# Second attention block: the last V chunk and the first output units cut in halves and placed between the head pairs, Q and K transposed into four PSUM banks each, scores in one pair of banks

## What is computed

```python
q, k, v = jnp.split(h @ w_qkv, 3, axis=-1)            # h 256 x 1024, w_qkv 1024 x 3072
q = rms_norm_2(to_heads(q), q_norm_g); k = rms_norm_2(to_heads(k), k_norm_g)   # 16 heads of 64
s = einsum(q, k) / 8 - slope[head] * dist             # causal: -inf above the diagonal
out = softmax(s) @ v                                  # 256 tokens are one block: plain causal attention
return out @ w_o                                      # w_o 1024 x 1024
```

## Time and profile before

| | us |
|---|---|
| median of 3 runs (lowest, highest) | 1060.16 (1060.11, 1060.77) |
| the profiled execution, its own time | 1060.12 |
| its span, first to last instruction | 1058.3 |
| PE busy in the span | 1030.8 (97%) |
| DVE, ACT, POOL busy | 712.5, 496.4, 110.3 |
| first Q transpose | at 789.40 |
| first scores, last values of a head pair | at 809.00, at 852.29 |
| last output matmul starts | at 864.18 |

### The profile page before, as it was taken

How to read it: one execution, slowest core, us unless ns; L and a number is a source line. 1 busy time by engine, 2 the same in 40 slices (tenths; PEclk the granted TensorE clock), 3 DMA queues, 4 the chain that set the end, 5 groups by cost and what they waited for, 6 DMA issues and landing times.

```text
span 1058.3 us, 16734 instructions
## 1 busy us (share of the span) xinstructions
PE 1030.8 (97%) x6774; PEld 907.4 (86%) x6774; DVE 712.5 (67%) x877; ACT 496.4 (47%) x565; POOL 110.3 (10%) x81
## 2 busy tenths in 40 slices
PE   8999998999999999999999999999997899999998
PEld 8987776799999998986899999998876689999997
DVE  6868646887667778754887656778674566545563
ACT  6455436454344436431564344436454655443440
POOL 1040002000010002025000010000000401000010
PEclk9999999899999999999999999999999899999999
DMA  8974346639787883694539778882652425655541
GB/s 320 371 261 141 120 127 218 236 110 345 260 274 281 272 279 126 203 288 133 194 134 350 269 265 284 268 282 92 238 162 78 159 81 199 192 191 179 193 160 40
DMA packets 119019, 221.62 MB, mean 209 GB/s; under 512 B 6510, under 2 KB 21040, under 8 KB 118960
## 3 DMA queue, kind: packets, MB, share of 16 engines
q1 hardware_dynamic: 117152, 214.97, 59.9%
q0 software_dynamic: 1680, 5.79, 1.7%
q10 hardware_dynamic: 128, 0.03, 0.0%
HBM read 215.07 MB, written 1.05 MB: 204 GB/s over the span
## 4 chain that ended last, share of the span: by engine, by line
PE 86%; DVE 7%; ACT 4%; issue 2%; DMA 0%; POOL 0%; SPq 0%; DVEq 0%; ACTq 0%
PE ps L459 81%; PE ps L1073 2%; ACT hi L356 1%; DVE lo L367 1%; PE ps L922 1%; DVE X L901 1%; PE ps L799 1%; DVE stat L2154 1%; PE ps L1422 0%; ACT aS L1858 0%; DVE aS L2149 0%; DMA X<-in_x 0%; ACT gate L1760 0%; DVE y_tmp L900 0%; PE ps L530 0%
## 5 line engine op out<-in xcount | busy, mean ns | idle before, releaser
L367 DVE TENSOR_TENSOR lo<-raw,hi 128x2048 fp32r<-128x2048 f32 x151 | 346.4, 2302 | 249.1 <-ACT hi L356 248.2
L356 ACT ACTIVATE hi<-raw 128x2048 fp32r<-128x2048 f32 x151 | 288.6, 1914 | 309.5 <-PE ps L459 291.4
L459 PE MATMUL ps<-hTh,hi 128*128 128x256 f32 x992 | 264.9, 285 | 0.9 <-DVE lo L367 0.6
L459 PE MATMUL ps<-hTh,lo 128*128 128x256 f32 x992 | 262.9, 283 | 0.0
L459 PE MATMUL ps<-hTl,hi 128*128 128x256 f32 x992 | 261.6, 283 | 0.0
L459 PEld LDWEIGHTS ps<-hTh,hi 128*128 128x128 f32 x992 | 182.4, 192 | 2.6 <-issue 1.4
L459 PEld LDWEIGHTS ps<-hTh,lo 128*128 128x128 f32 x992 | 182.5, 192 | 0.0
L459 PEld LDWEIGHTS ps<-hTl,hi 128*128 128x128 f32 x992 | 182.0, 192 | 0.2
L459 PE MATMUL ps<-hi,hidh 128*128 128x512 f32 (+1 forms) x424 | 164.6, 388 | 0.4 <-DVEq L794 0.4
L459 PE MATMUL ps<-hi,hidl 128*128 128x512 f32 (+1 forms) x424 | 163.7, 386 | 0.0
L459 PE MATMUL ps<-lo,hidh 128*128 128x512 f32 (+1 forms) x424 | 163.7, 386 | 0.0
(11 more groups left out here) (242 smaller groups left out, 886.3 us busy)
## 6 DMA issues: line engine op xcount, KB each, us to landing
raw<-in_mlp_w SPq DMA_DIRECT2D x64, 1024.0 KB, 5.3
ada_raw<-in_ada_w SPq DMA_DIRECT2D x44, 1024.0 KB, 7.4
raw<-in_w_in SPq DMA_DIRECT2D x20, 1024.0 KB, 7.8
raw<-in_w_ff_in SPq DMA_DIRECT2D x16, 1024.0 KB, 5.4
raw<-in_w_ff_out SPq DMA_DIRECT2D x16, 1024.0 KB, 5.2
raw<-in_attn_w_qkv SPq DMA_DIRECT2D x12, 1024.0 KB, 5.7
raw<-in_conv_w_in SPq DMA_DIRECT2D x8, 1024.0 KB, 5.8
taps<-u_pad SPq DMA_DIRECT2D x64, 71.0 KB, 4.9
```

What stands on the lines that cost most here:

```text
L356: nc.scalar.activation(hi[:, slot], raw[:, slot], ACT.Copy).then_inc(hi_made, 1)
L367: nc.vector.tensor_tensor(lo[:, slot], raw[:, slot], hi[:, slot].bitcast(F32), ALU.subtract).then_inc(lo_made, 1)
L459: return nc.tensor.matmul(o, lhs, rhs, start=start, stop=False, skip_group_check=True)
```

## The change

The same products, exponentials and copies are made. The order on PE, ACT and DVE and some PSUM banks change, and the 24 small matmuls L799 of the pipeline go. Q's transposes go between the two units of V chunk 4, K's behind it, into four banks each. V chunk 5 is split by token tile into four halves of 12 matmuls (`last_values`), in front of the scores of pairs 0, 1, 2 and 4. The pipeline is one step shorter: transposes of pair s-2, values of pair s-3. The output units (0,0) and (0,1) are cut in token halves too (`out_tile`) and go into steps 8, 9, 10 and behind them. Scores of all pairs use banks 5 and 7 and wait for `s_arg` of the pair just before. On DVE the reciprocals of pair s-1 now stand between the arguments and the maxima of pair s; the weight splits of units U_QKV+9 to +11 move into the pair loops of ACT and DVE.

```diff
@@ block.tensor
+        QKV_BANK = (0, 2, 0, 2, 4, 0)
+        QK_BANK = ((6, 7, 0, 1), (2, 3, 6, 7))
+        def value_bank(k):
+            return ((4, 6) if k < 4 else (0, 1))[k % 2]
...
-            qkv(4)
-            qk_transposes(Qs, 0)
-            qkv(5, lambda: qk_transposes(Ks, 4))
+            qkv(4, q_transposes)
+            pe.wait_ge(qk_kept, 4)
+            pe.wait_ge(qk_T, 2)
+            qk_transposes(Ks, 1)
+            pe.wait_ge(qk_T, 4)
+            def last_values(h, tt):
+                unit_tile(U_QKV + 10 + h, tt, 4 * h, ps[:, tt], h == 0)
+            def out_tile(c, tt):
+                unit_tile(U_WO + c, tt, 0, y_bank(tt, c, 4), True, need=56 if c == 0 and tt == 0 else None)
...
-                    if s >= 2:
-                        pe.wait_ge(s_arg, 2 * (s - 1))
-                        b, r = 4 + 2 * (s % 2) + i, slice(HD * i, HD * i + HD)
-                if s < 2:
-                    stay_warm((8, 4)[s], bank=1)
+                    pe.wait_ge(s_arg, 2 * s)
+                    b, r = 5 + 2 * i, slice(HD * i, HD * i + HD)
...
+            filler = {0: (0, 0), 1: (0, 1), 2: (1, 0), 4: (1, 1)}
+            for s in range(PAIRS + 3):
+                if s in filler:
+                    last_values(*filler[s])
                 if s < PAIRS:
+                    pair_scores(s)
+                elif s == PAIRS:
+                    pe.wait_ge(hT_lo, 56 + 3)
+                    out_tile(0, 0)
+                elif s == PAIRS + 1:
+                    out_tile(0, 1)
+                else:
                     pe.wait_ge(s_arg, AT_HEADS)
-                    out_unit(0, 0)
-                if s == PAIRS + 2:
-                    out_unit(0, 1)
-            out_unit(1, 0)
-            out_unit(1, 1)
+                    out_tile(1, 0)
+                if 2 <= s < PAIRS + 2:
+                    pair_transposes(s - 2)
+                if s >= 3:
+                    pair_values(s - 3)
+            out_tile(1, 1)
++            for c in range(2):
+                unit_x(pe, U_WO + 2 + c, None, hTh, hTl, 4, lambda tt, _, c=c: y_bank(tt, c, 4), False,
+                       need=56 if c == 0 else None, tail=TAIL_BANK[4] if c == 1 else None)
@@ block.vector
+                if s:
+                    pair_recip(s - 1)
+                dve.wait_ge(s_arg, 2 * s + 2)
...
+                if s == 1:
+                    dve_step(dve, U_QKV + 9)
...
+                if s == 4:
+                    dve_step(dve, U_QKV + 10)
+                if s == PAIRS + 1:
+                    dve_step(dve, U_QKV + 11)
```

More of the change, by code:

```diff
@@ L1599, in qkv, with unit_tile, qk_transposes @@
                     unit_x(pe, U_QKV + 2 * c + h, None, hTh, hTl, 4 * h,
-                           lambda tt, _: ps[:, chunk_bank(c) + tt], h == 0)
+                           lambda tt, _: ps[:, QKV_BANK[c] + tt], h == 0)
                     if h == 0:
                         between()
-            def qk_transposes(src, first):
-                pe.wait_ge(qk_n, 1 + first // 4)
+            def unit_tile(u, tt, k0, o, first, need=None):
+                slot, t = slot_of(u, None), slice(tt * P, (tt + 1) * P)
+                pe.wait_ge(lo_made, u + 1)
+                wh = hi[:, slot].rearrange("p (k n) -> p k n", k=4)
+                wl = lo[:, slot].rearrange("p (k n) -> p k n", k=4)
+                for k in range(4):
+                    if need is not None:
+                        pe.wait_ge(hT_lo, need + k0 + k + 1)
+                    mm(pe, o, hTh[:, k0 + k, t], wh[:, k], first and k == 0)
+                    mm(pe, o, hTl[:, k0 + k, t], wh[:, k])
+                    last = mm(pe, o, hTh[:, k0 + k, t], wl[:, k])
+                if tt == TT - 1:
+                    last.then_inc(used, 1)
+            def qk_transposes(src, which):
+                pe.wait_ge(qk_n, which + 1)
                 for f in range(4):
-                    if first + f >= 2:
-                        pe.wait_ge(qk_T, first + f - 1)
                     for k in (2 * f, 2 * f + 1):
@@ L1611, in qk_transposes @@
                             at = (k % 2) * SEQ + tt * P
-                            last = nc.tensor.transpose(ps[:, 6 + f % 2, at:at + P],
+                            last = nc.tensor.transpose(ps[:, QK_BANK[which][f], at:at + P],
                                                        src[:, tt, k * P:(k + 1) * P], ident)
@@ new lines, in pair_transposes, with pair_values @@
+            def pair_transposes(k):
+                pe.wait_ge(s_p, 2 * k + 2)
+                if k:
+                    pe.wait_ge(s_pT, k)
+                for i in range(2):
+                    for q in range(3):
+                        c = slice(q * P, (q + 1) * P)
+                        last = nc.tensor.transpose(ps[:, 2 + i, c], aS[:, k % 4, i, c], ident)
+                last.then_inc(s_tr, 1)
+            def pair_values(k):
+                pe.wait_ge(s_pT, k + 1)
+                if k % 4 >= 2:
+                    pe.wait_ge(hT_lo, 56 + k - 1)
+                elif k >= 4:
+                    pe.wait_ge(qk_kept, 6)
+                o = ps[:, value_bank(k)]
+                for i in range(2):
+                    r, v = slice(HD * i, HD * i + HD), slice((2 * k + i) * HD, (2 * k + i + 1) * HD)
+                    mm(pe, o[r, 0:SEQ], Vs[:, 0, v], aT[:, k % 2, i, 0:SEQ], True)
+                    last = mm(pe, o[r, P:SEQ], Vs[:, 1, v], aT[:, k % 2, i, SEQ:384])
+                last.then_inc(s_o, 1)
@@ L1678, in _ @@
+            out_tile(1, 1)
+            for c in range(2):
+                unit_x(pe, U_WO + 2 + c, None, hTh, hTl, 4, lambda tt, _, c=c: y_bank(tt, c, 4), False,
+                       need=56 if c == 0 else None, tail=TAIL_BANK[4] if c == 1 else None)
             norm_pe(pe, 5)
```

171 lines of the change are left out of this document (80 added, 91 removed).

## The result

The changed kernel takes **1049.92 us** (median of 1049.90, 1049.94, 1049.01 and 1052.55) against 1060.13 (four runs in turn with it): ratio 0.9908, 95% interval 0.9896 to 0.9920. Forecast were 1047.8 us and a range of 1045.0 to 1051.6: sign and range hold, but the gain is 10.2 us instead of 12.35, and the likeliest case's own range (1046.3 to 1049.3) is missed by 0.6.

The account below looks back on a forecast made before the run. PE bounds the kernel, busy 1030.8 of 1058.3 us. Removed 17.2, less 0.75 for starts and 5.3 for new waits, plus 1.2 at X's update, gives 12.35 us: 1047.8 from 1060.12, range 1045 to 1051.6.

Parts of the forecast that it names:

- the likeliest case: Whole kernel: the forecast schedule as it stands, give or take 1.5 us, 1046.3 to 1049.3 us; chance 0.70.
- Removed: PE in the attention stretch: 11.1 us of waits, 3.2 of L799 matmuls and 2.93 of slow clock go, together 17.2.
- the slow stretch: PE from 820 to 826: 5.86 us busy at half clock would be 2.93 shorter, if the clock stays up.
- Halves and unit starts: V and output units on PE: five more starts at 0.15 add 0.75 us; a half takes 2.87.
- One pair of banks: Scores of all pairs: they wait for the pair just before; forecast without serial pairs, as exponentials and maxima overlap the next scores.
- the rival of pairs in series: Pair loop: a pair takes 5.3 us instead of 2.5, waits 10.9 instead of 5.3, total 1053.4; chance 0.07.
- X's update: Behind the attention: DVE starts on time behind unit (1,0), its last part following PE by about 0.1; 1.2 us more gained.
- The waits left, 5.3 us: PE at scores 3, transposes 1, step 5, scores 6, transposes 4 and 5: new waits of 5.3 us, bounds 0 and 8.1.
- the ring: Pair loop: exponentials 1.90, reciprocals 0.1 and maxima 1.38 make 3.4 us a pair, against PE's own 2.5.
- The last wait: Transposes 5 in the pair loop: PE waits 0.95 us behind POOL.
- Granted clock 1.00 from 797 to 850: Sign of being right: PE's clock stays full there; 0.50 between 818 and 832 would show the forecast wrong.
- The first rival: Last pairs: clock falls, output halves run at half clock some 6 us and lose about 3, 1050.8 us; chance 0.15.

Follow-up runs that it names:

- run 7: Kernel before with only the transposes of Q and K changed: four banks each, Q between chunk 4's units, K behind them; 1055.60 us (0.9959).
- run 10: Changed kernel with all four V halves ahead of the pairs and the three output halves behind them; 1060.66 us (1.0003).
- run 12: Changed kernel with two DVE weight splits one step earlier and the reciprocals put back behind the scaling; 1050.39 us (0.9910).
- run 8: Kernel before with only the scores of all pairs put in one pair of banks; 1059.62 us (0.9998).
- run 2: Changed kernel with the scaling of the maxima on ScalarE instead of VectorE; 1049.79 us (0.9904).
- run 5: Changed kernel with the scaling of the maxima on ScalarE and two VectorE weight splits one step earlier; 1047.61 us (0.9887).
- run 9: Changed kernel with scaling on ScalarE, two VectorE splits one step earlier, and ScalarE's copy of V chunk 5 and a split moved later; 1046.39 us (0.9867).
- run 6: Changed kernel with 15 extra unused matmuls filling PE's waits ahead of scores 3, scores 6 and that step's transposes; 1049.38 us (0.9899).
- run 4: Changed kernel with 27 extra unused matmuls ahead of scores 3, scores 6 and that step's transposes; 1049.13 us (0.9899).
- run 1: Changed kernel with the reciprocals of the pair before put between maxima and scaling instead of ahead of the maxima; 1053.86 us (0.9937).
- run 11: Kernel before with only the reciprocals put early, ahead of the maxima; 1068.75 us (1.0082).
- run 3: Changed kernel with two of VectorE's weight splits one step earlier; 1048.99 us (0.9897).

## Why the prediction was right, and where it was not

- **Removed: two terms right, the third not.** The waits at Q and K (4.3 us counted, 4.5 measured in run 7) and L799 are gone. The 2.93 us for the slow stretch were counted on the condition that the clock stays up; it fell again (below).
- **Halves and unit starts: right.** A V half takes 795.72 - 792.80 = 2.92 us, forecast 2.87 (seven halves: 2.88 to 2.96). With the early reciprocals in place the halves carry the change: 10.7 us by run 10. The parts don't add up, and the early reciprocals alone cost 8.4 in the old order; so a part of the 10.7 may be no more than cover for them. Run 12, with late reciprocals and the halves, is only 5.2 us below run 7, which has late reciprocals, the new transposes and no halves. No run has the whole change with late reciprocals and without halves.
- **One pair of banks: right as far as tested.** In the old order it costs nothing (run 8: 0.9998, 0.9989 to 1.0007), against the rival of pairs in series. The rule of the Trainium skill that the forecast set beside that rival (Perfetto Trace Analysis, section "Optimizing Tensor Performance": independent groups of matmuls should rotate through banks) would have it cost time; run 8 measured none, and the measurement decides. In the new order 3.2 us of waits stand at scores 3 and 6, which wait for the arguments of the pair just before; whether a second pair of banks would save them or only move them was not run.
- **X's update: right.** DVE starts it directly behind unit (1,0). The last output matmul ends at 855.53 instead of 864.46, 8.9 us earlier (forecast 11), and the MLP starts 10.1 us earlier (860.22 instead of 870.36); the difference is the 1.2.
- **The waits left, 5.3 us: the sum right, the terms not; this step failed.** By place 0.8, 1.0, 0.1, 1.4, 1.0 and 0.95 were forecast; 1.41, 0.84, 0.47, 1.80, 0.84 and 0 came. That they add up to 5.36 is luck. The ring was put together from rows of the kernel before, where the scaling ran ahead of POOL, 0.17 us long. With the reciprocals moved ahead of it, it is held until POOL ends, and the ring is 3.83 us instead of 3.4. At scores 6 this is the miss: with the scaling on ScalarE the wait is 1.39 (run 2), as forecast. At scores 3 the arguments end at 806.43, as forecast, although the scaling ahead of them was held; but PE was there 0.6 us sooner than forecast (805.08 instead of 805.7), since the 16 transposes of Q, and those of K, took 1.67 us instead of 2.06. The 0.47 stand in runs 2, 5 and 9 too, where the scaling is not held: there the 0.1 was simply too small. The last wait is missing because PE was at half clock; at full clock it is 1.28 (run 6), so the term is about 5.36 + 1.28 = 6.6, that is 1.3 more.
- **Granted clock 1.00 from 797 to 850: wrong.** It was 0.51 from 822 to 828, which the forecast had named as a sign of being wrong. The first rival's mechanism came, in size not: it priced 3 us, and 0.5 to 0.9 was paid (runs 4 and 6), since PE would have waited for some of that time. By the rule of the Trainium skill that the forecast set beside it (TensorE: Matmul & The Clock Gate, section "A second HAM failure mode: psum-queue depth-cycling": short idle spells between groups of matmuls that cycle through banks can make the clock fall, there told of bf16 matmuls) it was to come; the trace agrees in so far as the clock fell, once, with no single wait over 1.80 us ahead of it. That the banks have a part in it, no run here shows.
- **Sum.** 12.35 - 1.3 - 0.9 = 10.15 against the 10.2 measured. So close it is partly luck: 1.28 and 0.9 are from the one trace of run 6, and two smaller differences were not forecast. The transposes of Q and K, without their waits, took 2.02 and 2.04 us before and take 1.67 and 1.66 now (0.7 gained), and the seven halves together took 0.4 longer than 7 x 2.87. With them it is 10.4.

That the scaling waits for POOL is shown by runs 1, 2, 11 and 12, in both orders. That it costs time is seen in the two traces of runs 5 and 3, 1.2 us of the stage; the medians, 1.4 apart, point the same way, but are not clear of the noise, and run 2 against the changed kernel shows 0.1.

## What to carry to other kernels

A duration taken from a trace holds for the neighbours that the operation had there: when a change moves the instruction that releases another engine, look up which of the two then runs into the other, in both directions. Where a loop is bound by a ring over several engines, filling the engine that waits can bring more (10.7 us here, with the early reciprocals in the ring) than a wait removed (4.5 at Q and K). Work of other loops on the ring's engines, such as a split or a late copy, is worth moving out of the steps without filler: run 9, which did that and put the scaling on ScalarE, is 3.5 us below the changed kernel. Half clock in a stretch where the engine would have waited anyway can cost far less than half of the stretch: 0.5 to 0.9 of 6 us here.

## What the runs showed of the hardware

POOL's multiplication (1.61 us alone) and two kinds of DVE's operations shut each other out, and the instruction that starts first runs to its end. A scaling of four columns took 0.59 to 0.66 us instead of 0.17; a split with both inputs in SBUF took 2.84 (run 2) and 2.89 (run 5) instead of 2.28 behind POOL; and POOL's two instructions took 3.57 (run 12) and 3.64 (run 1) behind a split, 3.66 (run 1) with a split between them. DVE's maxima took 1.11 to 1.14 with and without POOL at work, its arguments, one input of which is in PSUM, 1.01 (run 2) beside POOL and 1.02 alone, and ScalarE's scaling 0.20 and 0.21. The Trainium skill, SBUF — State Buffer, section "Who interferes with whom", says this of the port pair that VectorE and GpSimd share: `tensor_scalar` can take it, an operation with two SBUF inputs contends with GpSimd's reads, a reduction never does, and issue order decides who blocks. The traces agree on each point.
